# Stage entries of a two-block transformer kernel: where high and low parts, evictions and one copy stand on their engines

## What is computed

```python
for l in range(DEPTH_2):
    proj = jnp.einsum('bld,de->ble', h, w_in[l])
    a, g, zc, q, k, v, za, qi, ki, wi = jnp.split(proj, IN_SPLITS, axis=-1)
    y_conv = conformer_conv_branch(a, g, zc, ...)          # silu(layer_norm(conv)) * silu(zc)
    ...
    y_attn = dsa_sparse_attention(q, k, v, qi, ki, wi, topk) * jax.nn.silu(za)
    y = jnp.einsum('ble,ed->bld', jnp.concatenate([y_conv, y_attn], axis=-1), w_out[l])
    h = layer_norm(DEEPNORM_ALPHA * h + y, post_ln_g[l], post_ln_b[l])
```

## Time and profile before

| | |
|---|---|
| median of 3 runs | 922.79 us |
| the profiled execution | 922.45 us |
| its span | 920.6 us |
| granted TensorE clock | 0.995 |
| busy share: PE, DVE, ACT, POOL | 96%, 54%, 52%, 67% |

### The profile page before, as it was taken

One profiled execution on the slowest core, in us unless ns is written; L12 is line 12 of the kernel. 1 busy time (PEld: TensorE's weight loads), 2 busy tenths in 40 slices (PEclk: granted clock), 3 DMA queues, 4 the chain that ended last, 5 costly groups with the idle time before them and its releaser, 6 DMA issues.

```text
span 920.6 us, 17060 instructions
## 1 busy us (share of the span) xinstructions
PE 881.6 (96%) x6817; PEld 841.0 (91%) x6817; DVE 501.7 (54%) x1090; ACT 474.6 (52%) x930; POOL 617.8 (67%) x360
## 2 busy tenths in 40 slices
PE   5999999999999999999999999999998999999986
PEld 4995999999999898999999998999987989999776
DVE  3304111599828637655331115878954658799545
ACT  5425755633356446544444444445657554456672
POOL 4712655655556997999998897776854777766142
PEclk9999999999999999999999999999999999999998
DMA  8522743443432455455655672654220627544201
GB/s 269 173 80 92 231 135 97 133 138 93 138 102 96 158 195 183 133 189 185 199 157 169 190 209 83 204 172 138 101 93 1 183 60 213 157 138 160 70 1 46
DMA packets 134478, 128.09 MB, mean 139 GB/s; under 512 B 6496, under 2 KB 132064, under 8 KB 134400
## 3 DMA queue, kind: packets, MB, share of 16 engines
q1 hardware_dynamic: 133920, 126.20, 44.3%
q10 hardware_dynamic: 480, 0.79, 0.2%
HBM read 125.80 MB, written 1.05 MB: 138 GB/s over the span
## 4 chain that ended last, share of the span: by engine, by line
PE 83%; DVE 7%; POOL 4%; ACT 4%; DMA 1%; issue 1%; DVEq 0%; ACTq 0%
PE PS L605 22%; PE PS L607 22%; PE PS L606 22%; PE PS L832 3%; POOL w_lo L1146 3%; PE PS L596 2%; PE PS L972 1%; PE PS L742 1%; DVE PS L2019 1%; PE PS L794 1%; PE PS L1032 1%; DMA ring<-in_w_in 1%; ACT w_hi L1269 1%; POOL y_lo L1156 1%; PE PS L790 1%
## 5 line engine op out<-in xcount | busy, mean ns | idle before, releaser
L1146 POOL TENSOR_TENSOR w_lo<-ring,w_hi 128x1024 fp32r<-128x1024 f32 (+1 forms) x235 | 539.5, 2310 | 253.8 <-ACT w_hi L1269 243.3
L605 PE MATMUL PS<-x_hi,w_hi 128*128 128x256 f32 (+2 forms) x1560 | 459.5, 295 | 10.9 <-ACT zoneB L1252 4.8
L607 PE MATMUL PS<-x_hi,w_lo 128*128 128x256 f32 (+2 forms) x1560 | 444.9, 285 | 0.0
L606 PE MATMUL PS<-x_lo,w_hi 128*128 128x256 f32 (+2 forms) x1560 | 443.9, 285 | 0.0
L605 PEld LDWEIGHTS PS<-x_hi,w_hi 128*128 128x128 f32 (+1 forms) x1560 | 294.9, 189 | 16.0 <-issue 13.1
L606 PEld LDWEIGHTS PS<-x_lo,w_hi 128*128 128x128 f32 (+1 forms) x1560 | 294.4, 189 | 1.4 <-issue 0.2
L607 PEld LDWEIGHTS PS<-x_hi,w_lo 128*128 128x128 f32 (+1 forms) x1560 | 294.5, 189 | 0.0
L1269 ACT ACTIVATE w_hi<-ring 128x1024 fp32r<-128x1024 f32 (+2 forms) x233 | 235.5, 1014 | 80.7 <-PE PS L607 77.4
L2019 DVE SCALAR_TENSOR_TENSOR PS<-zoneA,cols,PS 128x256 f32<-128x256 f32 x240 | 98.7, 482 | 0.1
L1252 ACT ACTIVATE zoneA<-PS 128x272 f32<-128x272 f32 (+3 forms) x76 | 29.3, 386 | 108.7 <-PE PS L607 108.7
L1252 ACT ACTIVATE zoneB<-PS 128x256 f32<-128x256 f32 (+4 forms) x115 | 40.9, 378 | 75.9 <-DVE PS L1986 38.3
(11 more groups left out here) (290 smaller groups left out, 1205.1 us busy)
## 6 DMA issues: line engine op xcount, KB each, us to landing
ring<-in_w_in SPq DMA_DIRECT2D x58, 1024.0 KB, 5.5
ring<-in_w_ffn_in SPq DMA_DIRECT2D x22, 1024.0 KB, 5.1
ring<-in_w_out SPq DMA_DIRECT2D x12, 1024.0 KB, 5.0
ring<-in_w_ffn_out SPq DMA_DIRECT2D x16, 704.0 KB, 4.5
ring<-in_w_mla_o SPq DMA_DIRECT2D x4, 1024.0 KB, 5.0
ring<-in_w_hg_o SPq DMA_DIRECT2D x4, 1024.0 KB, 5.0
ring<-in_w_kv_b SPq DMA_DIRECT2D x2, 1024.0 KB, 5.3
ring<-in_w_q_b SPq DMA_DIRECT2D x2, 768.0 KB, 4.8
```

The source lines that it names most:

```text
L605: mm(out_, hi_w, hi_x, start=start, stop=False)
L606: mm(out_, hi_w, lo_x, start=False, stop=False)
L607: return mm(out_, lo_w, hi_x, start=False, stop=stop)
L1146: sub(lo_w, src, hi_w, ALU.subtract).then_inc(sem("w_lo"), 1)
```

## The change

- `add_normed`: the first addition stands right behind the first product, and the second product behind it; before, two products stood first. The other additions keep one product ahead.
- The meta copy stands ahead of the reciprocal's wait.
- `turns_over` is called with 5 instead of 3 ahead of the feed-forward entry, and with 10 instead of 12 ahead of layer 0.
- At `wo`, the four convolution high parts go from ACT to DVE (`Y_ORDER`), the last gate chunk is evicted ahead of the Silu of the three other gate slices, and `z_chunks` moves one slice of the last gate chunk (layer 0) or two (layer 1) from the last step to the ones before it.
- At the layer 1 entry, ACT writes `x_hi` ahead of `hT`, and the low part of slice 0 is made by DVE (`l0`) from `zT`, bias and `x_hi`; POOL makes the other seven.

```diff
 for _c in range(DC):
-    PLN_DVE += [f"b{_c}"] + ([f"a{_c + 2}"] if _c + 2 < DC else [])
+    PLN_DVE += [f"b{_c}"] + (["l0"] if _c == 1 else []) + ([f"a{_c + 2}"] if _c + 2 < DC else [])
...
+Y_ORDER = ["y0", "y1", "hi0", "hi1", "y2", "y3", "hi2", "hi3"] + [f"y{_c}" for _c in range(CC, DC)]
+def y_at(l, name):
+    return len(Y_ORDER) * l + Y_ORDER.index(name) + 1
 def z_chunks(l, s):
...
     at = 0
-    for s_, steps in ((n - 2, 1), (n - 1, 1), (n, 1), (n + 1, 1), (n + 2, 4)) if l else ((n - 1, 1), (n, 1), (n + 1, 2), (n + 2, 4)):
+    for s_, steps in ((n - 2, 1), (n - 1, 1), (n, 2), (n + 1, 2), (n + 2, 2)) if l else ((n - 1, 1), (n, 2), (n + 1, 2), (n + 2, 3)):
         spread[s_] = [("za", 3, at, at + steps)]
...
             bank_free(CHUNK[part("ffi", 1)])
-            turns_over(3, BANK[CHUNK[part("ffi", 1)]])
+            turns_over(5, BANK[CHUNK[part("ffi", 1)]])
             chunks_together([part("ffi", c) for c in range(3)], X, META,
...
                 bank_free(CHUNK[part(f"{T}g", 1)])
-                turns_over((12, 10)[l], BANK[CHUNK[part(f"{T}g", 1)]])
-                chunks_together([part(f"{T}g", 0), part(f"{T}g", 1), part(f"{T}a", 0)], X, 0, x_ready(f"{T}h"))
+                turns_over(10, BANK[CHUNK[part(f"{T}g", 1)]])
+                chunks_together([part(f"{T}g", 0), part(f"{T}g", 1), part(f"{T}a", 0)], X, 0,
+                                x_ready("L0h") if l == 0 else
+                                lambda i: pe.wait_ge(sem("lo_L1h"), i) if i else pe.wait_ge(sem("pln_z"), pln(0, "l0")))
                 for n, m in (("a", 1), ("g", 2), ("g", 3), ("a", 2), ("a", 3)):
...
                 for c in range(DC):
-                    lo_x(f"{T}h", c, x_lo[:, c, :], hT[:, c, :], x_hi[:, c, :])
+                    if l == 0:
+                        lo_x("L0h", c, x_lo[:, c, :], hT[:, c, :], x_hi[:, c, :])
+                    elif c:
+                        pool.wait_ge(sem("h_post"), c + 1)
+                        sub(x_lo[:, c, :], hT[:, c, :], x_hi[:, c, :], ALU.subtract).then_inc(sem("lo_L1h"), 1)
                 if l == 0:
...
                 for c in range(DC):
-                    lo_x(f"{T}y", c, x_lo[:, c, q_from:L], ycat[:, c, q_from:L], x_hi[:, c, q_from:L])
+                    if c < CC:
+                        pool.wait_ge(sem("y"), y_at(l, f"hi{c}"))
+                    else:
+                        pool.wait_ge(sem(f"hi_{T}y"), c - CC + 1)
+                    sub(x_lo[:, c, q_from:L], ycat[:, c, q_from:L], x_hi[:, c, q_from:L], ALU.subtract)\
+                        .then_inc(sem(f"lo_{T}y"), 1)
                 lo_piece(SPLIT[f"{T}wo1", 1])
...
                                 .then_inc(sem("meta_q"), 1)
-                def split_y(c):
-                    if c == 0:
-                        act.wait_ge(sem("chunk_done"), CHUNK[f"{T}za1", 1] + 1)
-                    split(f"{T}y", c, x_hi[:, c, q_from:L], ycat[:, c, q_from:L], (sem("y"), DC * l + c + 1))
                 def dsa_attention(i):
...
                     if s == DSA_N[l] + DSA_LAG:
-                        for c in range(CC + 1):
-                            if c < CC:
-                                act.wait_ge(sem(f"{T}cln_scaled"), c + 1)
-                                af(ycat[:, c, q_from:L], acc[:, c, q_from:L], ACT.Silu, scale=vec("conv_ln_g_2", 4 * l + c),
-                                   bias=vec("conv_ln_b_2", 4 * l + c)).then_inc(sem("c_silu"), 1)
-                            if c:
-                                split_y(c - 1)
-                        out_of_psum(act, *part(f"{T}za", 2))
-                        af(sza[:, 0:3, q_from:L], sza[:, 0:3, q_from:L], ACT.Silu).then_inc(sem("z_gates"), 1)
+                        for c in range(CC):
+                            act.wait_ge(sem(f"{T}cln_scaled"), c + 1)
+                            af(ycat[:, c, q_from:L], acc[:, c, q_from:L], ACT.Silu, scale=vec("conv_ln_g_2", 4 * l + c),
+                               bias=vec("conv_ln_b_2", 4 * l + c)).then_inc(sem("c_silu"), 1)
                     for n, m, _, end in z_chunks(l, s):
...
                              ACT.Silu if last else ACT.Copy, n=n_q, ahead=not last)
+                        if last:
+                            out_of_psum(act, *part(f"{T}za", 2))
+                            af(sza[:, 0:3, q_from:L], sza[:, 0:3, q_from:L], ACT.Silu).then_inc(sem("z_gates"), 1)
                     if s == CLN_STEP[l] - 1:
...
-                act.wait_ge(sem("chunk_done"), CHUNK[f"{T}za1", 1] + 1)
                 for c in range(CC, DC):
-                    split_y(c)
+                    act.wait_ge(sem("y"), y_at(l, f"y{c}"))
+                    af(x_hi[:, c, q_from:L], ycat[:, c, q_from:L], ACT.Copy).then_inc(sem(f"hi_{T}y"), 1)
                 round_piece(SPLIT[f"{T}wo1", 1])
...
                     affine = dict(scale=1.0, bias=vec("post_ln_b_2", 8 * l + c))
+                    af(x_hi[:, c, :], zT[:, c, :], ACT.Identity, **affine).then_inc(sem(f"hi_L{l + 1}h"), 1)
                     af(hT[:, c, q_from:L], zT[:, c, q_from:L], ACT.Identity, **affine).then_inc(sem("h_post"), 1)
-                    af(x_hi[:, c, :], zT[:, c, :], ACT.Identity, **affine).then_inc(sem(f"hi_L{l + 1}h"), 1)
...
-                for c in range(DC + 1):
-                    if c < DC:
-                        g = CHUNK[name(c)]
-                        y = PS[:, BANK[g], PS_AT[g]:PS_AT[g] + SEQ]
-                        order[0] += 1
-                        v.scalar_tensor_tensor(out=y, in0=y, scalar=vec(gain, c), in1=nrm[:, 0, 0:SEQ],
-                                               op0=ALU.mult, op1=ALU.mult).then_inc(sem("dve_order"), 1)
-                    if c:
-                        g = CHUNK[name(c - 1)]
-                        y = PS[:, BANK[g], PS_AT[g]:PS_AT[g] + SEQ]
-                        dve.wait_ge(sem("dve_order"), order[0] - (c < DC))
-                        if by == "h_mid":
-                            out_of_psum(dve, "x", (c - 1) // 2)
-                        v.tensor_tensor(hT[:, c - 1, META:L], hT[:, c - 1, META:L], y, ALU.add).then_inc(sem(by), 1)
-                    if c > 1 and then:
-                        then(c - 2)
+                def bank_of(c):
+                    g = CHUNK[name(c)]
+                    return PS[:, BANK[g], PS_AT[g]:PS_AT[g] + SEQ]
+                def product(c):
+                    order[0] += 1
+                    v.scalar_tensor_tensor(out=bank_of(c), in0=bank_of(c), scalar=vec(gain, c), in1=nrm[:, 0, 0:SEQ],
+                                           op0=ALU.mult, op1=ALU.mult).then_inc(sem("dve_order"), 1)
+                def added(c, behind):
+                    dve.wait_ge(sem("dve_order"), order[0] - behind)
+                    if by == "h_mid":
+                        out_of_psum(dve, "x", c // 2)
+                    v.tensor_tensor(hT[:, c, META:L], hT[:, c, META:L], bank_of(c), ALU.add).then_inc(sem(by), 1)
+                product(0)
+                added(0, 0)
+                product(1)
+                for c in range(1, DC):
+                    if c + 1 < DC:
+                        product(c + 1)
+                    added(c, c + 1 < DC)
+                    if then:
+                        then(c - 1)
                 if then:
...
             add_squares("fpost")
+            link(v.tensor_copy(hT[:, :, 0:META], meta_rows[:, :].rearrange("p (c t) -> p c t", c=DC)))
             rstd("fpost", 1, nrm[:, 0, 0:SEQ])
-            link(v.tensor_copy(hT[:, :, 0:META], meta_rows[:, :].rearrange("p (c t) -> p c t", c=DC)))
             add_normed(lambda c: ("ffo", c), "ffn_post_g", "h_ready")
...
                 dve.wait_ge(sem("z_gates"), 2 * l + 1)
-                for c in range(CC):
-                    dve.wait_ge(sem("c_silu"), CC * l + c + 1)
-                    v.tensor_tensor(ycat[:, c, q_from:L], ycat[:, c, q_from:L], szc[:, c, q_from:L], ALU.mult)\
-                        .then_inc(sem("y"), 1)
+                for name in Y_ORDER[:2 * CC]:
+                    c = int(name[-1])
+                    if name[0] == "y":
+                        dve.wait_ge(sem("c_silu"), CC * l + c + 1)
+                        v.tensor_tensor(ycat[:, c, q_from:L], ycat[:, c, q_from:L], szc[:, c, q_from:L], ALU.mult)\
+                            .then_inc(sem("y"), 1)
+                    else:
+                        dve.wait_ge(sem("chunk_done"), CHUNK[f"{T}za1", 1] + 1)
+                        dve.wait_ge(sem("y"), y_at(l, f"y{c}"))
+                        v.tensor_copy(x_hi[:, c, q_from:L], ycat[:, c, q_from:L]).then_inc(sem("y"), 1)
                 dve.wait_ge(sem("z_gates"), 2 * l + 2)
...
                     normed_row(c)
+                    if c == 1:
+                        dve.wait_ge(sem(f"hi_L{l + 1}h"), 1)
+                        step("l0", v.scalar_tensor_tensor(out=x_lo[:, 0, :], in0=zT[:, 0, :],
```

(2 more changed lines are left out.)

## The result

| | before | after |
|---|---|---|
| median | 922.85 us (4 runs, 922.62 to 925.74) | 914.75 us (4 runs, 914.61 to 915.14) |
| profiled execution | 922.45 us | 914.61 us |
| its span | 920.6 us | 912.8 us |

The ratio is 0.9898 (95% interval 0.9882 to 0.9915). The four runs before are few: 86 more runs of the kernel before, beside the experiments on five chips, have a median of 925.05 (920.34 to 927.73), so the usual gain is nearer 10 us.

What follows compares the result with a forecast made beforehand. TensorE, on the chain of waits for 83% of the span, was taken as the bound, with time only at five idle entries. Terms summed to -6.5, 922.45 to 915.95, or 916.3 us on the median; range 914.9 to 918.8.

Steps and rivals of the forecast that it cites:

- layer 0 entry: First matmul of layer 0: with the copy ahead of the reciprocal, PE starts at 555.77 instead of 557.57, -1.8 us.
- feed-forward entry: Feed-forward's first matmul: the first addition no longer hides its wait, so the low part comes later, +0.1 us.
- layer 1 entry: Layer 1's first matmul: PE starts 0.67 earlier, but POOL's second slice takes part back, -0.4 us.
- projection, layer 0: Layer 0's output projection: earlier gate chunk eviction, then PE's own transposes bound it; no stall, -2.2 us.
- projection, layer 1: Layer 1's output projection: PE starts 2.9 earlier, about 0.7 given back at a late third slice, -2.2 us.
- sum of work: The five entry and projection terms added over the whole kernel, -6.5 us.
- rule of taking a start earlier by x as a kernel shorter by x: At all five places: an earlier PE start shortens the kernel equally, if the next slices come in time.
- the cut of two is needed: Ahead of layer 0: all twelve idle matmul calls would end at 556.19 and cost 0.4 us.
- casts held up: Rival at the output projections: each DVE cast costs the median 1.06 us; -4.3 us, 918.5, chance 0.12.
- slower: Rival at the output projections: casts beside a weight piece could each cost 2.46 us; 929.7, chance 0.03.
- Given back at the weights: Rival: PE arrives earlier at chunks whose low parts POOL makes at its own pace; 921.3, no change, chance 0.05.

Runs made afterwards that it cites:

- fill_all: Kernel before with idle matmuls in the gaps of both attention tails and ahead of both output projections; 920.80 us, ratio 0.9966.
- l1_entry_only: Kernel before with only the layer 1 entry as the change has it; 924.54 us, in an execution with half clock.
- turns12: Changed kernel with 12 instead of 10 idle matmul calls ahead of layer 0; feed-forward entry's first matmul to layer 0's took 194.22 us (changed kernel 194.26).
- piece_beside_casts: Changed kernel with an extra weight-piece-sized subtraction in POOL's order beside DVE's casts at both projections; 920.01 us, ratio 0.9954.
- copy_behind: Changed kernel with the meta copy behind the reciprocal again; 917.27 us (6 runs).
- fill_tails: Kernel before with idle matmuls in the gaps of the two attention tails alone; 924.58 us, ratio 0.9991.
- fill_entries: Kernel before with idle matmuls only ahead of the first matmul of both output projections; 922.77 us, ratio 0.9979.
- after_again: The changed kernel run once more, unaltered; 914.86 us (4 runs).
- norm_only: Kernel before with the change's addition order, meta copy and idle matmul calls, projections as before; 922.62 us, ratio 0.9987.
- idle_matmuls_in_gaps: Kernel before with two more idle matmul calls, in the two standstills of layer 0's attention tail only; 925.24 us, ratio 1.0003.
- old_slices_layer0: Changed kernel with the old spread of the last gate chunk in layer 0 alone; 915.35 us, ratio 0.9897 to the kernel before.
- hi23_act_ff: Changed kernel with projection high parts of slices 2 and 3 back on ACT and before's order at the feed-forward entry; 913.67 us (4 runs).
- best_filled: hi23_act_ff with idle matmuls added in the gaps of the two attention tails; 913.49 us.

## Why the prediction was wrong

By its own steps; the work is B and C against fill_all's 181.28 and 170.80, since before's B holds half clock.

| term | forecast | measured | from |
|---|---|---|---|
| layer 0 entry | -1.8 | -1.68 | A |
| feed-forward entry | +0.1 | +0.15 | 0.28 less 0.13 |
| layer 1 entry | -0.4 | -0.35 | l1_entry_only |
| projection, layer 0 | -2.2 | -2.29 | B, -2.93, of which -0.64 is the layer 1 start |
| projection, layer 1 | -2.2 | -2.3 | C, -2.01, and 0.29 given back from the layer 1 entry |
| sum of work | -6.5 | -6.5 | |
| clock | not there | -1.57 | before's B, 182.85 less 181.28 |

**The step that failed** is the base of the sum: "The profiled execution took 922.45 us and would take 915.95". It takes everything in that execution which the edits don't touch as kept, and the stretch at 699 to 703, worth 1.57 us of B, wasn't. The work forecast was right to about 0.1 us in every term. With 1.57 more, the forecast is 914.7; measured was 914.75. That these agree to 0.05 is luck: the beginnings alone vary by 1.8 us, the changed kernel has a stretch itself in some executions, and the forecast stood on 922.79, the first three runs of the kernel before, where the usual time is 925.05. As a gain, 6.5 was forecast and some 10 is usual, the rest being half clock as far as the experiments show. The rule of taking a start earlier by x as a kernel shorter by x held, at one clock.

- **The layer 0 entry**: as forecast; the copy is 1.43 of it. That "the cut of two is needed" was wrong (turns12).
- **The feed-forward entry**: 0.95 us of idle bracket where 0.7 was forecast, a slip of arithmetic: by the prediction's own numbers it is 1.67 + 0.1 - 2 x 0.45 = 0.87. The two calls cost nothing.
- **The layer 1 entry**: both halves right, the gain and what POOL's second slice takes back.
- **Projection of layer 0**: no stall, as forecast; the next bound is PE's own turning (no bracket at 702.70).
- **Projection of layer 1**: the third slice was 0.45 late (878.22, behind 876.33 + 4 x 0.36) instead of 0.7. All eight casts took 0.28 to 0.30 us, as taken.
- **Rivals**: "casts held up" and "slower" need a weight piece beside the casts. None stands there, and piece_beside_casts shows that a cast is held beside one, at 2605 ns, but not that the kernel would lose what the rival counted. "Given back at the weights" isn't seen: C and the time behind both entries kept what they gained.
- **The width**: the range was made from bounds of work alone, and its lower end doesn't come out of its own terms: 916.3 less 0.7 and 0.27 is 915.3, not 914.9. The kernel before itself ran from 920.34 to 927.73 in all comparisons together, which a forecast from one execution has to hold.

## What to carry to other kernels

Scan the granted clock over the whole span in short windows before summing terms, not the mean in the table (0.995 hid 1.57 us), and count work against an execution without lowered stretches. An edit that closes a standstill of 2 to 3 us of TensorE can be worth more than the standstill (between copy_behind and the changed kernel, 1.43 us of start and 2.4 of time); a few idle matmuls in the gaps give that part alone and make the times narrow. A high part moved from one engine to another should be looked at beside GpSimd's program order: here it was harmless until a long piece stood beside it, and then one cast took 2.6 us.

## What the runs showed that was not expected

- Granted half clock appeared behind single standstills of 1.75 and 1.99 us (fill_tails, copy_behind), and in a tail whose standstills are below 0.8 us each (before, fill_entries, after_again). It is not the same in each execution: before's standstill of 1.37 at layer 0 brought none in any profile, the changed kernel had a stretch in one profile of two at the same gaps, and in its own profile the kernel before had none at its largest standstills, 1.75 and 3.08, nor had norm_only at its 1.75. What decides it between these isn't settled.
- The sum over a stretch of each microsecond's missing share of the clock was 1.7 us, or twice that (3.4). In B it cost 1.50 to 1.57, and the long ones 2.6 to 2.7 (fill_tails and idle_matmuls_in_gaps against 181.28), so PE had a little slack to make up. In C it depends on where it falls: 1.57 at fill_tails' projection, but 0.79 and 0.70 in layer 1's tail (old_slices_layer0 against the changed kernel, hi23_act_ff against best_filled), and only 1.70 for the long one of idle_matmuls_in_gaps at 876 to 884.
- The beginning of the kernel, up to the feed-forward entry, takes between 360.71 and 362.48 us in these profiles, with nearly the same program up to there, which hides effects of some tenths unless intervals are compared.
